# First token attention: the scores of two units issued together in four score banks

## The reference

```python
def block(args):                                    # dsa_mixer, 32 queries at a time
    ...
    _, sel = lax.top_k(score, topk)                 # which keys each query sees
    logits = jnp.einsum('bqhd,bqkhd->bqhk', qb, k_sel).astype(jnp.float32) * scale
    logits = logits + bias                          # relative bias; -inf where not causal
    p = jax.nn.softmax(logits, axis=-1).astype(v.dtype)
    return jnp.einsum('bqhk,bqkhd->bqhd', p, v_sel)
...
y_attn = dsa_mixer(...) * jax.nn.silu(attn_z)
z = z * jax.nn.sigmoid(z @ w_glu + b_glu)           # end of the state space mixer
mod = cond @ w_ada[l] + b_ada[l]                    # shift, scale, gate
y = jnp.concatenate([y_ssm, y_attn], axis=-1) @ w_out[l]
x = x + gate[:, None, :] * y
```

## Time and profile before

| what | value |
|---|---|
| median of 3 runs | 1327.5 us (1327.26 to 1329.16) |
| the profiled execution, its own time | 1327.23 us |
| its span, first to last instruction | 1325.4 us |
| PE busy | 1293.7 us, 98% |
| DVE busy | 882.3 us, 67% |
| ACT busy | 364.8 us, 28% |
| POOL busy | 270.7 us, 20% |

### The profile page before, as it was taken

How to read it: one execution, slowest core, us unless ns; L and a number is a source line. 1 busy time by engine, 2 the same in 40 slices (tenths; PEclk the granted TensorE clock), 3 DMA queues, 4 the chain that set the end, 5 groups by cost and what they waited for, 6 DMA issues and landing times.

```text
span 1325.4 us, 16804 instructions
## 1 busy us (share of the span) xinstructions
PE 1293.7 (98%) x6016; PEld 874.0 (66%) x6016; DVE 882.3 (67%) x2050; ACT 364.8 (28%) x900; POOL 270.7 (20%) x264
## 2 busy tenths in 40 slices
PE   4999999999999999999999999999999999999998
PEld 3444555544544544886455556888888888888887
DVE  5898999679331465465456676676767767777563
ACT  4222121225200102232456676111223332330000
POOL 1168568215003287700000000000000000000000
PEclk9999999999999999999999999999999999999999
DMA  9773425651312112312103002212324224224210
GB/s 320 201 142 120 143 40 154 201 177 35 125 33 83 64 64 64 127 33 95 65 1 64 1 2 55 73 64 66 110 64 127 65 65 126 64 93 146 84 52 32
DMA packets 91038, 120.63 MB, mean 91 GB/s; under 512 B 16488, under 2 KB 52654, under 8 KB 90956
## 3 DMA queue, kind: packets, MB, share of 16 engines
q1 hardware_dynamic: 86256, 110.81, 27.3%
q10 hardware_dynamic: 2956, 5.05, 1.2%
q0 software_dynamic: 1744, 3.70, 0.9%
HBM read 111.00 MB, written 6.84 MB: 89 GB/s over the span
## 4 chain that ended last, share of the span: by engine, by line
PE 93%; DVE 3%; DMA 1%; issue 1%; ACT 1%; SPq 0%; POOL 0%; DVEq 0%; ACTq 0%; POOLq 0%
PE bank L1510 18%; PE bank L875 12%; PE bank L1536 10%; PE bank L888 9%; PE bank L1438 7%; PE bank L1396 6%; PE bank L910 5%; PE bank L1166 4%; PE bank L1276 4%; PE bank L1348 3%; PE bank L1376 3%; PE bank L1211 2%; PE bank L939 2%; PE bank L1481 2%; PE bank L1046 1%
## 5 line engine op out<-in xcount | busy, mean ns | idle before, releaser
L1510 PE MATMUL bank<-arena 128*128 128x256 f32 x1120 | 241.9, 379 | 0.0
L1510 PEld LDWEIGHTS bank<-arena 128*128 128x128 f32 x1120 | 212.8, 190 | 28.9
L875 PE MATMUL bank<-arena 128*128 128x512 f32 (+1 forms) x384 | 157.0, 565 | 0.0
L1536 PE MATMUL bank<-arena 128*128 128x256 f32 x616 | 133.1, 379 | 0.0
L888 PE MATMUL bank<-arena 128*128 128x512 f32 x288 | 127.7, 596 | 0.0
L1536 PEld LDWEIGHTS bank<-arena 128*128 128x128 f32 x616 | 117.0, 190 | 15.9
L910 PEld LDWEIGHTS bank<-arena 128*128 128x128 f32 (+2 forms) x660 | 77.7, 143 | 73.3 <-issue 45.7
L875 PEld LDWEIGHTS bank<-arena 128*128 128x128 f32 x384 | 71.9, 190 | 77.8 <-issue 73.6
L910 PE MATMUL bank<-arena 128*128 128x128 f32 (+2 forms) x660 | 93.1, 278 | 20.5 <-ACT arena L1620 9.0
L2924 DVE CUSTOM_DVE_ANT_0 arena<-bank,arena 128x128 f32<-128x128 f32 (+3 forms) x128 | 57.6, 487 | 66.3 <-PE bank L1348 65.0
L1438 PE MATMUL bank<-arena 128*128 128x256 f32 x448 | 97.6, 379 | 0.0
(11 more groups left out here) (388 smaller groups left out, 1945.5 us busy)
## 6 DMA issues: line engine op xcount, KB each, us to landing
arena<-in_w_in SPq DMA_DIRECT2D x14, 2048.0 KB, 8.1
arena<-in_w_up SPq DMA_DIRECT2D x20, 1024.0 KB, 7.0
arena<-in_w_ada SPq DMA_DIRECT2D x16, 512.0 KB, 8.7
arena<-in_w_down SPq DMA_DIRECT2D x8, 1024.0 KB, 7.4
arena<-in_w_out SPq DMA_DIRECT2D x2, 2048.0 KB, 9.9
arena<-in_w_attn_br SPq DMA_DIRECT2D x8, 512.0 KB, 8.2
arena<-in_w_o SPq DMA_DIRECT2D x2, 2048.0 KB, 7.7
rb_dram<-rb_one_dram ACTq DMA_DIRECT2D x1, 2560.0 KB
```

The source lines that it names most:

```text
L875: mm = pe.matmul(ps[:, 0:n], act[:, k, 128 * t:128 * t + 128], w[:, k, 0:n], start=(k == 0), stop=(k == kt - 1))
L1510: mm = pe.matmul(ps, left[:, k, :], right[:, k, :], start=(first and k == 0), stop=(k == 3), skip_group_check=True)
L1536: mm = pe.matmul(down_acc(i, name), left, right, start=first and name in ("P1", "P7", "P2", "P4"), stop=last, skip_group_check=True)
```

## The change

In the loop over the steps, PE waits at n = 0 for all four score banks instead of for two at n = 0 and two at n = 1. The scores of an odd unit are no longer issued in their own step, but in the step before, right behind the scores of the even unit and ahead of the fill, the turns and the values of that step. The program computes the same, with the same matmuls in the same banks; the other engines' programs are as before.

```diff
             for n in range(NS1 + 3):
-                if n < 2:
-                    first = 2 * ((n + (PBANK["az", 3] < 2)) % 2)
-                    for b in (first, first + 1):
+                if n == 0:
+                    for b in range(4):
                         pe.wait_ge(bank_free[b], before_sub1[b])
                 if n < NS1:
-                    pair_scores(n)
+                    if n % 2 == 0:
+                        pair_scores(n)
+                        pair_scores(n + 1)
                     pair_fill(n)
                 if n == NS1:
                     pe.wait_ge(lg_done, 2 * NS1)
```

## The result

The changed kernel takes 1331.96 us (median of 7 runs, 1331.61 to 1335.71) against 1327.26 us before (7 runs, 1326.76 to 1329.16): 4.7 us slower, ratio 1.004 with a 95% interval of 1.0029 to 1.0052. The prediction was 1329.1, with a range up to 1331.0 and a chance of 0.79 for no change that can be measured. It was wrong. The profiled execution took 1331.61 us, its span 1329.8, which is 4.4 more than before. One later execution of the kernel before, of 1515.99 us at a mean granted clock of 0.851, was in a slow state and is left out of all that follows.

A forecast was written before the change was run, and what follows sets the result against it. PE was busy 98% of the span and bounded everything behind the attention, while DVE paced most attention steps. A start 1.70 us late less 0.1 saved gave 1.6, added to 1327.5 for 1329.1 us, range 1327.3 to 1331.0.

The forecast's parts named there:

- The start: First units: scores 0 wait for all four banks, so DVE takes the first gate sum 1.70 us late.
- the saving of two sets of scores in a row: Scores of units 4 and 5 back to back save 0 to 0.16 us, taken as 0.1.
- my sum: Whole kernel: 1.70 us at the start less 0.1 saved, 1.6 us slower.
- The even steps: Turns and values stand behind the next unit's scores, 0.38 to 1.02 us later; slack covers it, so no cost.
- the waits inside: Steps 2 to 14: next scores wait for earlier logits with fill queued behind; taken as nothing, bound 1.02 us.
- The tail: Scores 15 leave the gap ahead of turns 13, which wait for ACT, not PE; nothing won.
- The rival for slower: Even steps: DVE waits for values delayed behind the next scores; 1330.1 to 1334.0 us, chance 0.16.
- the other rival: All eight pairs save 0.16 us each, 1.3 us, giving the delay back; 1327.2 to 1328.3 us, chance 0.18.

The follow-up runs named there:

- e6: Changed kernel with unread matmuls filling all of PE's long gaps at the start and in the tail: median 1329.69 us, ratio 1.0014.
- e8: Changed kernel with start and tail as before, score pairs only for units 2 to 13: median 1329.21 us, ratio 1.0005.
- e12: Kernel before with only scores 15 moved right behind scores 14: median 1330.27 us, ratio 1.0018.
- e2: Changed kernel with only scores 0 and 1 together behind the four-bank wait, later units each in their own step: median 1332.68 us, ratio 1.0026.
- e10: Changed kernel with unread matmuls filling PE's gaps in the first units alone, tail as changed: median 1332.61 us, ratio 1.0033.
- e4: Changed kernel with unread matmuls in two gaps, ahead of scores 0 and ahead of turns 13: median 1332.07 us, ratio 1.0027.
- e9: The changed kernel measured again, nothing altered: median 1331.72 us, ratio 1.0032.
- e1: Changed kernel with the start of the kernel before, pairs only from unit 2 on: median 1329.98 us, ratio 1.0012.
- e3: Changed kernel with scores 14 and 15 each in their own step: median 1332.89 us, ratio 1.0031.
- e11: Kernel before with unread matmuls of 512 and 256 columns ahead of scores 0, starting attention late without an added gap: median 1331.8 us, ratio 1.0023.
- e5: Kernel before with unread matmuls filling PE's gaps in the first units and the tail: median 1329.58 us, ratio 1.0006.
- e7: Changed kernel with the first gate sum issued ahead of the four-bank wait: median 1331.18 us, ratio 1.0015.

## Why the prediction was wrong

**The start: right.** I had the first gate sum 1.70 late on DVE. Against DVE's read of bank 0, which came 0.21 earlier in this execution (285.70 for 285.91), it was 1.34 + 0.21 = 1.55 late. The 0.15 that is missing is the saving of two sets of scores in a row, which I had kept to units 4 and 5: sixteen records of 128 columns took 287.04 - 286.45 = 0.59 from start to start instead of twice 0.38, that is 0.17 less. At full clock the changed kernel is 1.7 over before by the fit (0.5 to each side), and e6, which has its order and no fall in the attention, is 1.39 longer there, for the 1.6 of my sum.

**The even steps and the waits inside: right.** Behind unit 0 DVE waited for scores no more, and it waited for the values of unit 1 (L1134) in step 4, as forecast, only that this wait was 2.08 us, because the fill ahead of it ran at half clock. No other values were late between there and the tail, that stretch kept its length (36.16 us for 36.17, though it lay 2.84 later and not 1.6 to 1.7), and e8 has pairs 2 to 13 at no cost.

**The tail: the step that failed.** I wrote that scores 15 leave the gap ahead of turns 13, "and the gap only grows", "nothing won". The gap was priced at nothing because PE was waiting there anyway. The step that failed is that zero: I did not ask what PE's clock does behind a longer gap. e12 is that one edit: it has the gap of 1.76 us, the half clock from 335.7 on, and no execution at full clock. In the trace of the changed kernel it cost 1.56 us, in that of e12 1.57.

**The same omission in the first units.** I said PE would be idle some 1.5 us ahead of scores 0, and took every duration behind it from rows at full clock. The first half clock added 1.50. e2 has it without the other pairs, and the profiles of e6 and e10, with the gaps filled and the order unchanged, are without it; e4, with only the gap I had named filled, still has it, and is 1.64 us longer than e6 in the attention.

So the sum lacked two terms. In the trace of the changed kernel 1.34 at the start, 1.50 and 1.56 make 4.40, and the two profiled executions differ by 4.38. From three other kernels, over the attention: 1.39 for the late start less the savings (e6), 1.64 for the first half clock (e4 less e6) and 1.57 for the second (e12 less before) make 4.60, for 4.61 of the changed kernel. The medians differ by 4.7 in the first measurement and by 3.5 in e9, where the kernel before had falls of its own. The rival for slower had the right side with the wrong mechanism: it was late values by waiting, and no wait of that kind cost anything. The 1.3 us of the other rival, eight saved changes of mode, were there as spacing (0.17 at the start, 0.16 for 256 columns: in e1 the scores of units 4 and 5 took 295.36 - 294.33 = 1.03 for 1.19). In the paced steps they became more waiting: e8, with six of the pairs, gained 0.18 in all.

**What stays open.** Which gap decides in one execution, and how much is the gap and how much the lateness in the first units. e3 and e2 fell in the tail with the old gaps, e11 in the first units with the old gaps, and the kernel before fell short of 1.000 in 44 of 76 executions, of which no profile shows where. The profiles, one of each kernel, show no fall in a place whose gaps are all filled (e5, e6, the first units of e10), and that the gap of 1.76 us ahead of turns 13 came with a fall in the profile of every kernel that had it unfilled (changed, e1, e7, e9, e10, e12); none of their 52 executions is at 1.000. They do not show how idle PE may be, and when.

## What to carry to other kernels

An idle gap on TensorE is not free because the engine would have waited anyway: work moved out of a wait makes the wait longer, and the clock behind it can fall to half, at 1.5 us a time here. Before a change that moves matmuls together, add up PE's idle time ahead of each piece that paces the end, and look for the granted clock of single executions and not at the median alone. Where independent matmuls share one order, leave one in each gap, even if it is ready sooner: e12 against the kernel before is that choice. It is no guarantee, since e3 made it and its tail fell.

## What the runs showed of the hardware

The granted clock fell to half behind pauses of PE of 0.2 to 1.8 us each, with matmuls between them: ahead of the first fall PE was busy for 5.57 of 9.30 us, ahead of e11's fall near 297 for 7.02 of 8.80:

```profile
288.00:296.80 8.80, 7.02 (x57) 2.88 (x55) 6.49 (x28) 4.45 (x20) 2.24 (x4) 1.00 0.83 297
296.80:300.30 3.50, 3.50 (x9) 1.40 (x5) 2.74 (x9) 1.41 (x6) 1.99 (x3) 0.51 0.42 155
```

The busy share alone does not tell the two apart, since the kernel before, over nearly the same stretch of its attention, was no busier than e11 and stayed at full clock in its profile:

```profile
285.00:294.00 9.00, 7.12 (x56) 2.98 (x56) 7.71 (x32) 4.93 (x22) 2.94 (x5) 1.00 0.82 294
```

The half clock comes late: it lay for the most part over the dense work behind the gaps and not over the gaps (3.40 us busy of 3.40 in the changed kernel; 5.58 of 6.80 in e10). The Trainium skill, page "TensorE: Matmul & The Clock Gate", section "A second HAM failure mode: psum-queue depth-cycling", tells of a kernel in which frequent short idles between groups of matmuls made the clock swing between its two levels; this trace agrees, with falls at 294.3 and 338.6 us behind idles of at most 1.76 us. And sets of matmuls on quarter tiles (64x64) that follow each other save 0.16 to 0.17 us against sets with full tiles between them.
